# Part of an output projection taken between the attention heads and the norm of their second half

## The reference, cut to what matters

```python
h = rmsnorm(x, pre_mix_g)
q_a, k_a, v_a, q_b, k_b, v_b, f_b = split(h @ w_in)
o_a = swa_sink_attention(q_a, k_a, v_a, sinks)        # 16 heads of 64: columns 0:1024
o_b = forgetting_attention(q_b, k_b, v_b, log_f)      # 16 heads of 64: columns 1024:2048
o_a = rmsnorm(o_a, grp_swa_g)                         # each half has a norm of its own
o_b = rmsnorm(o_b, grp_fox_g)
mix = concatenate([o_a, o_b], -1) @ w_out             # 2048 x 2048
x = x + rmsnorm(mix, post_mix_g)
```

## Time and profile before

| what | us |
|---|---|
| median of 3 runs | 1681.36 (1681.15 to 1685.89) |
| the profiled execution's own time | 1682.97 |
| its span in the profile | 1680.9 |
| PE busy | 1644.2 |
| DVE busy | 1007.8 |
| ACT busy | 877.3 |

### The profile page before, as it was taken

The page is one execution under the profiler, slowest core; times in us unless marked ns, Lnnn a source line. Parts: engine busy times, 40 slices in busy tenths (PEclk is TensorE's granted clock), DMA queues, the critical chain, the costliest instruction groups (busy, mean ns, idle before and its releaser), DMA issues.

```text
span 1680.9 us, 28894 instructions
## 1 busy us (share of the span) xinstructions
PE 1644.2 (98%) x11198; PEld 1501.7 (89%) x11198; DVE 1007.8 (60%) x1437; ACT 877.3 (52%) x1264; POOL 21.8 (1%) x46
## 2 busy tenths in 40 slices
PE   8999999999999999999999999989999999999996
PEld 8989998879999999999998888878998888898885
DVE  5566667556666666666664444473666455776565
ACT  6355557446555554554453444354434695655455
POOL 3000000000000000000000000010000000000000
PEclk9999999999999999999999999999999999999999
DMA  7654541554666666666665665556566547655641
GB/s 232 203 157 140 162 139 45 193 163 153 192 189 188 187 193 200 200 199 190 197 213 177 200 205 189 175 149 169 166 180 176 162 147 245 185 176 176 195 155 64
DMA packets 154574, 295.09 MB, mean 176 GB/s; under 512 B 13428, under 2 KB 15624, under 8 KB 153592
## 3 DMA queue, kind: packets, MB, share of 16 engines
q1 hardware_dynamic: 153512, 289.76, 55.7%
q0 software_dynamic: 944, 4.14, 0.7%
q10 hardware_dynamic: 32, 0.01, 0.0%
HBM read 291.51 MB, written 2.10 MB: 175 GB/s over the span
## 4 chain that ended last, share of the span: by engine, by line
PE 95%; DVE 2%; ACT 1%; issue 0%; DMA 0%; ACTq 0%; SPq 0%; DVEq 0%
PE bank L1487 29%; PE bank L1489 29%; PE bank L1488 29%; PE upper L1629 1%; PE upper L1632 1%; ACT junk L522 1%; PE upper L1543 1%; PE bank L1543 1%; PE upper L1646 1%; PE upper L1762 1%; DMA x_tok<-in_x 0%; PE upper L1659 0%; PE upper L1660 0%; PE upper L1806 0%; PE upper L1658 0%
## 5 line engine op out<-in xcount | busy, mean ns | idle before, releaser
L891 DVE TENSOR_TENSOR w_lo<-raw,w_hi 128x1024 fp32r<-128x1024 f32 (+1 forms) x548 | 654.5, 1209 | 530.5 <-ACT w_hi L464 529.0
L464 ACT ACTIVATE w_hi<-raw 128x1024 fp32r<-128x1024 f32 (+1 forms) x548 | 568.3, 1049 | 573.4 <-PE bank L1489 567.4
L1487 PE MATMUL bank<-hT_hi,w_hi 128*128 128x256 f32 x2272 | 632.0, 278 | 1.3 <-DVE hT_lo L922 1.3
L1488 PE MATMUL bank<-hT_lo,w_hi 128*128 128x256 f32 x2272 | 629.1, 277 | 0.0
L1489 PE MATMUL bank<-hT_hi,w_lo 128*128 128x256 f32 x2272 | 629.0, 277 | 0.0
L1487 PEld LDWEIGHTS bank<-hT_hi,w_hi 128*128 128x128 f32 x2272 | 427.0, 188 | 2.6 <-issue 1.7
L1488 PEld LDWEIGHTS bank<-hT_lo,w_hi 128*128 128x128 f32 x2272 | 427.5, 188 | 0.0
L1489 PEld LDWEIGHTS bank<-hT_hi,w_lo 128*128 128x128 f32 x2272 | 426.8, 188 | 0.0
L1487 PE MATMUL bank<-w_hi,hT_hi 128*128 128x512 f32 x672 | 264.7, 394 | 0.0
L1489 PE MATMUL bank<-w_hi,hT_lo 128*128 128x512 f32 x672 | 261.8, 390 | 0.0
L1488 PE MATMUL bank<-w_lo,hT_hi 128*128 128x512 f32 x672 | 261.5, 389 | 0.0
(11 more groups left out here) (347 smaller groups left out, 1080.1 us busy)
## 6 DMA issues: line engine op xcount, KB each, us to landing
raw<-in_w_in SPq DMA_DIRECT2D x180, 512.0 KB, 3.8
raw<-in_w_up SPq DMA_DIRECT2D x176, 512.0 KB, 4.5
raw<-in_w_down SPq DMA_DIRECT2D x80, 512.0 KB, 4.6
raw<-in_w_out SPq DMA_DIRECT2D x64, 512.0 KB, 4.3
raw<-in_w_xkv SPq DMA_DIRECT2D x16, 512.0 KB, 4.5
raw<-in_w_down SPq DMA_DIRECT2D x16, 256.0 KB, 3.1
raw<-in_w_xq SPq DMA_DIRECT2D x8, 512.0 KB, 3.9
raw<-in_w_xo SPq DMA_DIRECT2D x8, 512.0 KB, 4.6
```

The costliest lines, as they stand in the source:

```text
L464: act.activation(w_hi[:, s, at:at + n], raw[:, s, 0:n], ACT.Copy).then_inc(hi_ready, 1)
L891: dve.tensor_tensor(w_lo[:, s, at:at + n], raw[:, s, 0:n], w_hi[:, s, at:at + n].bitcast(F32), ALU.subtract).then_inc(lo_ready, 1)
L1487: pe.matmul(o, l_hi, r_hi, start=start, stop=False, skip_group_check=True)
L1488: pe.matmul(o, l_hi, r_lo, start=False, stop=False, skip_group_check=True)
```

## The change

The sliding half gets a mean, root and reciprocal of its own, at the heads 22 and 23, and DVE scales its columns there. Its eight chunks are turned by PE and split by ACT and DVE behind head 24, into places of their own (`sT_hi`, `sT_lo`). The groups of `w_out` become two half groups for the rows of the sliding half (`w_out_a`, 4 pieces each), two half groups for the rows of the forgetting half (`w_out_b`), which go on in the same banks, and two whole groups. Behind head 34 PE takes three pieces of the first half group at once, then turns the eight chunks of the forgetting half, then goes on with the fourth piece. ACT and DVE split the pieces from the fourth on (index 3) behind their part of the phase. `stay_warm` ahead of the phase goes away. `mix_gain` moves to a place in `kbT`, and its load waits until all scores are made.

```diff
 # ACT, head(i)
+                if i == 22:
+                    act.wait_ge(swa_mean, 1)
+                    act.activation(half_stat(0), half_stat(0), ACT.Sqrt).then_inc(swa_root, 1)
 # DVE, head(i)
+                if i == 22:
+                    dve.wait_ge(squares, 4)
+                    dve.tensor_scalar(half_stat(0), half_stat(0), 1.0 / D_SWA, EPS, ALU.mult, ALU.add).then_inc(swa_mean, 1)
+                if i == 23:
+                    dve.wait_ge(swa_root, 1)
+                    dve.reciprocal(half_stat(0), half_stat(0)).then_inc(swa_rstd, 1)
+                    dve.wait_ge(swa_rstd, 1)
+                    for c in range(2):
+                        for b in range(NB):
+                            dve.tensor_scalar(work[:, b, c * W:(c + 1) * W], work[:, b, c * W:(c + 1) * W], head_factor(b, c), None,
+                                              ALU.mult).then_inc(scaled, 1)
 # ACT and DVE, behind the groups of w_in
+            early = FIRST_PIECE[GROUP["w_out_a"][0]]
             for i in range(24, 2 * NH + 3):
                 head(i)
+                if i == 24:
+                    out_phase(range(8))
 # ACT
+            act.wait_ge(mean_ready, 2)
+            act.activation(half_stat(1), half_stat(1), ACT.Sqrt).then_inc(root_ready, 1)
             scale_part(work, work, 2, head_factor)
-            phase(1)
+            out_phase(range(8, KC))
+            for j in range(8):
+                split(early + j + SLOTS - 1)
 # DVE
-            rstd(2, 1, 10, D_SWA, 4)
-            scale_rows(work, work, head_factor)
-            phase(1)
+            for b in range(NB):
+                dve.tensor_scalar(work[:, b, 2 * W:3 * W], work[:, b, 2 * W:3 * W], head_factor(b, 2), None, ALU.mult).then_inc(scaled, 1)
+            out_phase(range(8, KC))
+            for j in range(8):
+                split(early + j + SLOTS - 1)
 # PE
             for i in range(24, 2 * NH + 3):
                 head(i)
-            stay_warm(4, 16)
-            phase(1, work, 6, 4)
-            with pe.Fori(0, 2) as i:
-                for e in range(2):
-                    group(GROUP["w_out"][e], "tok", i, 16, first=1 if e == 0 else None)
+                if i == 24:
+                    out_phase(range(4))
+            for j in range(BEFORE):
+                out_piece(GROUP["w_out_a"][0], j, 0)
+            out_phase(range(4, 8))
+            for j in range(BEFORE, 8):
+                out_piece(GROUP["w_out_a"][j // 4], j % 4, 0)
+            for g in GROUP["w_out_b"]:
+                for j in range(4):
+                    out_piece(g, j, 8)
+            for g in GROUP["w_out"]:
+                pe.wait_ge(banks_free, evacuated(g - 2))
+                for j in range(8):
+                    out_piece(g, j, 0)
 # POOL
+            pool.wait_ge(scores_done, 2 * NH)
             pool.dma_start(mix_gain[:, :], A["post_mix_g"][0].partition_broadcast(P)).then_inc(gain_loaded, 16)
```

More of the change, by code:

```diff
@@ L60 @@
     [("kv_a", 4), ("q_a", 8), ("q_a", 8), ("v_b", 8), ("v_b", 8), ("q_b", 8), ("k_b", 8), ("q_b", 8), ("k_b", 8)]
-    + [("w_out", 8)] * 4 + [("w_up", 8)] * 22 + [("w_down", 24)] * 4
+    + [("w_out_a", 4)] * 2 + [("w_out_b", 4)] * 2 + [("w_out", 8)] * 2 + [("w_up", 8)] * 22 + [("w_down", 24)] * 4
     + [("gla_qk", 8), ("gla_v", 8)] + [("sb_q", 8)] * 2 + [("sb_k", 8)] * 2 + [("sb_v", 8)] * 2
@@ L70 @@
 TOTAL = FIRST_PIECE[-1]
+EVACUATIONS = [sum(0 if name == "w_out_a" else 2 for name, _ in PLAN[:g]) for g in range(len(PLAN) + 1)]
 DOWN = [2] * 20 + [1] * 4
+BEFORE = SLOTS - 1
 ROOM = 64
@@ L79 @@
 PIECE_AT = [AT.get(g, 0) for g, (_, n) in enumerate(PLAN) for _ in range(n)]
-for _name, _before in (("w_up", "w_out"), ("w_down", "w_up"), ("xq", "w_out2")):
+for _name, _before in (("w_down", "w_up"), ("xq", "w_out2")):
     for _j in range(SLOTS - 1):
@@ L94 @@
 PHASES = ["pre_mix", "grp", "pre_ffn", "norm_mix_2", "norm_mem_2", "out_norm_2", "norm_xattn_2"]
-READER = [GROUP[n][0] for n in ("kv_a", "w_out", "w_up", "gla_qk", "xk", "w_out2", "xq")]
+READER = [GROUP[n][0] for n in ("kv_a", "w_out_a", "w_up", "gla_qk", "xk", "w_out2", "xq")]
 def pair_bank(n, q):
     p = 2 * (READER[n] % 2)
+    if n == 1:
+        return [p, p + 1, 2 - p, 3 - p, 4, 5, 6, 7][q]
     return [p, p + 1, 4, 5, 6, 7, 2 - p, 3 - p][q]
@@ L271, in st, with half_stat, out_t @@
             return stat[:, 4 * k:4 * k + n]
+        def half_stat(half):
+            return stat[:, 4:8].rearrange("p (b k) -> p b k", k=2)[:, :, half]
+        def out_t(c):
+            return (sT_hi[:, c, :], sT_lo[:, c, :]) if c < 8 else (hT_hi[:, c, :], hT_lo[:, c, :])
         def head_factor(b, c):
@@ L331, in _ @@
                 group(w_in, col, g)
-            with sp.Fori(0, 2) as i:
-                for e in range(2):
-                    group(A["w_out"][0], i * (2 * W) + e * W, GROUP["w_out"][e], i, 16)
+            w_out = A["w_out"][0]
+            for e in range(2):
+                group(w_out[0:D // 2, :], e * W, GROUP["w_out_a"][e], pieces=(2,) * 4)
+            for e in range(2):
+                group(w_out[D // 2:D, :], e * W, GROUP["w_out_b"][e], pieces=(2,) * 4)
+            for e in range(2):
+                group(w_out, (2 + e) * W, GROUP["w_out"][e])
             with sp.Fori(0, 11) as i:
@@ L633, in x_squares @@
                                (junk if k == 3 else junk2)[:, 0:D // 2])
-            with act.Fori(0, 2) as i:
-                for e in range(2):
-                    g = GROUP["w_out"][e]
-                    if e == 0:
-                        act.wait_ge(squares, 10)
-                    group(g, i, 16, take=lambda g=g, e=e: squares_out(g, i, junk, e))
-                    act.wait_ge(banks_free, evacuated(g) + i * 4)
+            act.wait_ge(squares, 10)
+            for e, g in enumerate(GROUP["w_out_b"] + GROUP["w_out"]):
+                group(g, take=lambda g=g, e=e: squares_out(g, 0, junk, e))
+                act.wait_ge(banks_free, evacuated(g))
             root(3, 2, mean_ready, root_ready)
@@ L1096, in _ @@
             dve.wait_ge(gain_loaded, 16)
-            with dve.Fori(0, 2) as i:
-                for e in range(2):
-                    g = GROUP["w_out"][e]
-                    group(g, i, 16, take=lambda g=g, e=e: gained_out(work, mix_gain, g, i, e, e))
+            for e, g in enumerate(GROUP["w_out_b"] + GROUP["w_out"]):
+                group(g, take=lambda g=g, e=e: gained_out(work, mix_gain, g, 0, e, e))
             def residual(n, k, src, m, done):
@@ L1113, in residual @@
                 total_squares(k + 1, 2)
-            residual(3, 2, work, evacuated(GROUP["w_out"][3]), 14)
+            residual(3, 2, work, evacuated(GROUP["w_out"][1]), 14)
             rstd(4, 3, 14, D)
```

54 lines of the change are left out of this document (47 added, 7 removed).

## The result

| | before | changed |
|---|---|---|
| median of 4 runs each | 1681.89 (1681.15 to 1685.89) | 1696.22 (1692.84 to 1696.8) |
| ratio, 95% interval | | 1.0075 (1.006 to 1.0091) |
| the profiled execution's own time | 1682.97 | 1692.84 |
| its span | 1680.9 | 1690.7 |

The changed kernel is slower, as forecast, but by about twice the sum: 1696.22 lies above the range, whose end was 1692.0. The same kernel was timed again in three later sets, each beside the kernel before: 1.0051, 1.0067 and 1.0059.

A forecast was written before the change was run, and what follows sets the result against it. PE was taken as the bound (95% of the chain), with DVE nearly full in the heads. Heads +7.6, gap -3.5 and clock +3.2 gave +7.3 us: 1690.3 profiled, 1688.7 us as median, range 1682.5 to 1692.

The forecast's parts named there:

- Sqrt at head 22: ACT's Sqrt table load and root delay the last split, the copies into `kbT` and head 23: +1.2 us.
- Exp again: Exp table load at head 23, begun when the row maxima are there: 1.28 us, hidden; uncovered 1.3.
- Scaling: DVE's reciprocal and four scales of the sliding half at head 23, ahead of head 24's bias: +1.9 us.
- The early half: Eight chunks behind head 24, DVE waiting for ACT's first chunk, then eight remainders: head 25 and all behind +4.7 us.
- Rival B: In the heads PE is the bound and DVE's work sinks into it: not slower, sum -1.3 us; chance 0.12.
- Three pieces and the late half: Between heads and projection, 9.5 us become 6.0 between piece 2 and piece 3, PE standing 3.8: -3.5 us.
- The plan, at nothing: Projection's straight code, same 384 matmuls, loads and banks, costs nothing; 1 us if fetching the code came late.
- The clock: One half-speed stretch of about 3.2 us in the heads and one in the tail, 1.6 us each: +3.2 us.
- Rival C: Exp load uncovered, or a second slow stretch at one place: +8.6 to +10.5 us, 1690 to 1692; chance 0.13.
- The level: Whole kernel: +7.3 us on the profiled 1682.97 gives 1690.3; the median, 1.6 below, gives 1688.7 us.

The follow-up runs named there:

- e4_no_root: Changed kernel with the sliding half's root replaced by a copy, so no Sqrt or Exp table load at heads 22 and 23: 1690.85 us, ratio 1.0049.
- e2_two_before: Changed kernel with two pieces instead of three ahead of the late transposes: 1687.72 us, ratio 1.0029.
- e8_split_first: Changed kernel with two pieces ahead of the late transposes and piece 3 split by ACT and DVE before their late chunks: 1688.51 us, ratio 1.0037.
- e12_all_behind: Changed kernel with both halves of the phase behind head 34 and no pieces ahead of the late half: 1689.21 us, ratio 1.0039.
- e1_again: Changed kernel as it is, timed again in set 1 beside the kernel before: 1690.77 us, ratio 1.0051.
- e15_again: Changed kernel as it is, timed again in set 4 beside the kernel before: 1693.96 us, ratio 1.0059.
- e9_late_two: Changed kernel with early-half quads behind heads 31 to 34, two pieces ahead of the late transposes, piece 3 split before the late chunks: 1681.76 us, ratio 0.9994.
- e5_late: Changed kernel with the early half of the phase in four quads behind heads 31 to 34 instead of behind head 24: 1686.60 us, ratio 1.0030.
- e6_fill: Changed kernel with 13 and 16 constant matmuls in PE's two waits at head 26: 1689.76 us, ratio 1.0049.
- e14_fill_both: Changed kernel with constant matmuls in all three PE waits, 13 and 16 at head 26, 31 before piece 3: 1688.67 us, ratio 1.0027.

## Why the prediction was wrong, step by step

*Sqrt at head 22*, +1.2: 0.9 at `kbT` in the profile, 1.1 to 1.4 by `e4_no_root`. Right. The load of 246.46 ended at 247.74 and the root began at 247.76. The further 1.38 us of drain that the Trainium skill ("ScalarE: Activation LUTs", "What ACT_TABLE_LOAD costs") adds are not there this time either.

*Exp again*, hidden: right in its price, wrong in its reason. The load did not stand behind the wait; it ran ahead of it, in ACT's idle time.

*Scaling*, +1.9: head 24 went from 0.9 to 2.7 us late, 1.8. Right. What it can bring on besides, a low clock behind PE's wait of 1.46 us, was not thought of; in the changed kernel PE had the early transposes at that place.

*The early half*, +4.7: head 25 went from 2.7 to 7.2 late, 4.5. ACT's chunks began 2.6 us into head 24 (255.09 to 257.70), the first remainder 0.85 behind them, eight took 3.23. Together +7.2, where the forecast had 7.6. Rival B is out: DVE was the bound, and what it was given came through whole.

*Three pieces and the late half*, -3.5: piece 3 came 5.9 us after the first transpose (forecast 6.0), PE stood for 4.02 (3.8). `e2_two_before` and `e8_split_first` confirm the place.

*The plan, at nothing:* right, by `e12_all_behind`.

*The clock*, +1.6 and +1.6: **this is the step that failed.** The places were right, the two waits in the heads too (1.98 and 1.97 us, forecast 1.8 and 2.2). The size was taken from the two places read in the trace of before, 3 us at 0.50 in each, as if that were a property of the clock. The same waits were followed by 3.4 us in `e1_again` and 6.8 in the changed kernel's profile and in `e15_again`, and in the last a third stretch lay under the drained heads and the pieces, where no wait was longer than 0.48 us. The term measured 3.2, 4.6, 4.6 and 8.1 in four traced executions. Its upper bound, twice the forecast, was 6.4 and thus too low as well. Rival C, "a second slow stretch at one place", named the mechanism, with a chance of 0.13 for it and the Exp load together; by the forecast's own price of 1.6 a stretch it would end at 10.2 with both, not at the 10.5 that it states. There were up to three stretches, each up to twice as long.

*The level.* The sum, 1690.3 for the profiled execution, was 2.5 below its 1692.84, and of this the term of the clock explains 1.4 (4.6 - 3.2) and the stretch at 1618.6 about as much. Then 1.6 was subtracted for the median, as before; but here the profiled execution was the shortest of four. The measured time would have been inside the range in one set of four (1690.77) and outside in the others; which of them came first was luck.

Open: what decides in one execution whether none, 3.4 or 6.8 us of low clock follow the same wait. No run here tells it. Open too is where the low clock was in the three untraced executions of the first set; `e15_again` is an execution of their length, not one of them.

## What to carry to other kernels

Extra work for a full engine goes where that engine has gaps (here the drained heads, 5.9 us earlier at the first matmul), and if two engines hand it on, the second takes it one step later, or each portion costs the handover again. Whoever fills a gap with prepared work keeps one portion for the gap that the filling makes behind itself. Count PE's waits twice over, once for the wait and once for the half clock behind it, and give the second a wide range, for one trace shows one case of it.

## What the runs showed of the hardware

The granted clock fell at two waits of 2 us with 0.5 us of work between them (PE busy for 0.99 of the 4.40 us from 259.8 on), in the changed kernel before the second had ended (263.1 against 263.73), not only behind one unbroken gap. How long it stayed low differed between executions of the same program: 3.4 us in the heads in one, 6.8 in three. It could fall, or not, behind one and the same wait of 1.46 us (`e9_late_two` and `e5_late`). When one low stretch was filled away, the next could be longer (6.8 us in `e6_fill` at the stall, 3.4 in the changed kernel's profile) or turn up elsewhere (276.9 to 283.8 in `e14_fill_both`).

An activation table was loaded at 250.71, ahead of the wait of the instruction that needed it at 253.13, while in the kernel before a load came behind such a wait (1187.59). Idle time of ACT hid it.
